# Position bias of the prompt attention added on TensorE by an identity product, with maximum and exponentials read from PSUM

## What is computed

```python
def diff_attention(q, k, v, tq, ts, lam, subln_g, lam_init):
    s = jnp.einsum('bqhjd,bshjd->bhjqs', q, k).astype(jnp.float32) * HEAD_DIM ** -0.5
    dist = jnp.abs(tq[:, None] - ts[None, :]).astype(jnp.float32)
    bias = -alibi_slopes(H_A)[:, None, None] * dist[None]
    mask = (ts[None, :] // CHUNK) <= (tq[:, None] // CHUNK)
    s = jnp.where(mask, s + bias[:, None], NEG)
    p = jax.nn.softmax(s, axis=-1)
    a = p[:, :, 0] - lam * p[:, :, 1]
    o = jnp.einsum('bhqs,bshe->bqhe', a.astype(v.dtype), v)
    o = rms_norm(o, subln_g) * (1.0 - lam_init)
```

## Time and profile before

| what | value |
|---|---|
| median of 3 runs | 1322.1 us (1322.06 to 1329.15) |
| the profiled execution, its own time | 1323.07 us |
| its span, first to last instruction | 1321.3 us |
| mean granted PE clock over the span | 0.917 |
| `attention_prompt`, from PE's first matmul to ACT's last copy | 298.18 to 368.5 us |

### The profile page before, as it was taken

One profiled execution on the slowest core, in us unless ns is written; L12 is line 12 of the kernel. 1 busy time (PEld: TensorE's weight loads), 2 busy tenths in 40 slices (PEclk: granted clock), 3 DMA queues, 4 the chain that ended last, 5 costly groups with the idle time before them and its releaser, 6 DMA issues.

```text
span 1321.3 us, 23547 instructions
## 1 busy us (share of the span) xinstructions
PE 1033.8 (78%) x8385; PEld 657.7 (50%) x8386; DVE 427.7 (32%) x815; ACT 239.2 (18%) x478; POOL 218.1 (17%) x361
## 2 busy tenths in 40 slices
PE   4899899986576699983787788877877878766865
PEld 3888788875565344542344444444433444433432
DVE  4523324338843113874411111111111121101118
ACT  3222212336455000110110101010100111100100
POOL 0002102000100000201222222222231223212211
PEclk9899999996799799997799889899898998978988
DMA  9587666521063793075689699987999988899955
GB/s 350 173 298 256 223 236 216 184 95 48 1 226 112 274 272 115 32 301 201 215 291 386 229 382 395 370 326 272 408 375 387 328 303 299 308 398 404 396 220 216
DMA packets 97912, 347.52 MB, mean 263 GB/s; under 512 B 15057, under 2 KB 20225, under 8 KB 73146
## 3 DMA queue, kind: packets, MB, share of 16 engines
q1 hardware_dynamic: 81258, 311.56, 63.7%
q0 software_dynamic: 13856, 30.13, 6.9%
q10 hardware_dynamic: 2736, 4.98, 1.0%
HBM read 329.15 MB, written 29.52 MB: 271 GB/s over the span
## 4 chain that ended last, share of the span: by engine, by line
PE 27%; DMA 16%; issue 6%; DVE 2%; SPq 1%; ACT 0%; POOL 0%; POOLq 0%; DVEq 0%; ACTq 0%
PE PS L1771 8%; DMA hT<-h_rows,ixo 7%; DMA W<-w 7%; PE PS L1786 6%; PE PS L1802 4%; PE PS L1827 4%; PE PS L1841 2%; PE PS L1777 1%; DMA vec<-ln_b 1%; PE PS L1759 1%; PE PS L1817 1%; DVE hido L1893 0%; PE PS L1794 0%; DVE hid L1888 0%; DMA W<-expert_rows 0%
## 5 line engine op out<-in xcount | busy, mean ns | idle before, releaser
L1771 PE MATMUL PS<-W,XT 128*32 128x256 f32 x2048 | 130.0, 410 | 48.5 <-DMA W<-w 26.5
L1786 PE MATMUL PS<-W,XTo 128*64 128x256 f32 x1216 | 139.5, 381 | 0.0
L1771 PEld LDWEIGHTS PS<-W,XT 128*32 128x32 f32 x2048 | 80.1, 118 | 114.8 <-issue 90.6
L1786 PEld LDWEIGHTS PS<-W,XTo 128*64 128x64 f32 x1216 | 93.2, 137 | 44.0 <-issue 10.6
L1802 PE MATMUL PS<-W,hidTo 128*64 128x512 f32 x304 | 90.7, 722 | 16.3 <-DVE hidTo L1896 10.7
L431 DVE TENSOR_TENSOR w_lo<-raw,w_hi 128x2048 fp32r<-128x2048 f32 x26 | 59.5, 2288 | 126.1 <-ACT w_hi L371 126.1
L305 PE MATMUL PS<-w_hi,u_hi 128*128 128x512 f32 x240 | 94.4, 393 | 1.7 <-DVE w_lo L431 1.7
L305 PE MATMUL PS<-w_hi,u_lo 128*128 128x512 f32 x240 | 93.5, 389 | 0.0
L305 PE MATMUL PS<-w_lo,u_hi 128*128 128x512 f32 x240 | 93.4, 389 | 0.0
L1827 PE MATMUL PS<-W,hidT 128*32 128x512 f32 x512 | 72.1, 677 | 26.3 <-issue 24.3
L1856 ACT ACTIVATE sg<-PS 64x256 f32<-64x256 f32 x32 | 12.1, 378 | 346.9 <-PE PS L1771 346.9
(11 more groups left out here) (338 smaller groups left out, 1497.8 us busy)
## 6 DMA issues: line engine op xcount, KB each, us to landing
W<-w SPq DMA_DIRECT2D x192, 1024.0 KB, 13.9
raw<-w_in SPq DMA_DIRECT2D x26, 1024.0 KB, 9.2
oaT<-w_ada SPq DMA_DIRECT2D x8, 1536.0 KB, 8.6
W<-expert_rows SPq DMA_DIRECT2D x24, 512.0 KB, 12.5
obT<-w_ada SPq DMA_DIRECT2D x8, 512.0 KB, 8.9
kc<-cache_k_diff SPq DMA_DIRECT2D x8, 512.0 KB, 4.8
vc<-cache_v_diff SPq DMA_DIRECT2D x8, 512.0 KB, 3.5
Wa<-p_a SPq DMA_DIRECT2D x4, 1024.0 KB, 7.5
```

Of the source, the lines that this page charges most:

```text
L1771: mm = pe.matmul(PS[64 * h + 32 * c:64 * h + 32 * c + 32, UP_B + i, 0:F], XT[:, i, k, 32 * c:32 * c + 32], t.W13[:, 2 * i + c, h, k], star ...
L1786: mm = pe.matmul(PS[64 * h:64 * h + 64, XH_B, 0:F], XTo[:, k], t.W13[:, slot, h, k], start=k == 0, stop=k == KD - 1)
```

## The change

The scores come out of PSUM complete. Before each product of queries and keys, PE now multiplies the identity (stationary) by the bias (moving, 128 or 256 columns) into the same place of PSUM (`start=True, stop=False`), and the scores are accumulated on it. The factor SM goes into the queries: ACT's eviction of `qT` multiplies by it, and `b_col` is multiplied by it once by a new small DVE instruction, for which ACT waits (`bias_scaled`). In `logits` the two instructions of L773 are gone: the maximum is taken straight from PSUM. The exponentials read PSUM as well and write `L`. With that the waits move: `scores(n)` and `logits(n)` wait for the exponentials of group n-2 (`exp_done`), and the exponentials of group n wait for `a_done` of group n-2, since they are what writes `L` now. In `attention_sample` the multiply-and-add becomes an add.

```diff
--- before.py
+++ after.py
@@ -142,7 +142,7 @@
         ada2_in, ada2_mm, ada2_ev = sem("ada2_in"), sem("ada2_mm"), sem("ada2_ev")
         mod_out = [sem(f"mod2_out{i}") for i in range(2)]
         brow_in = [sem(f"brow_in{i}") for i in range(2)]
-        bin_in = sem("bin_in")
+        bin_in, bias_scaled = sem("bin_in"), sem("bias_scaled")
         g_add, g_sig = sem("g_add"), sem("g_sig")
         g_out = [sem(f"g_out{i}") for i in range(2)]
         hi_done, lo_done, half0_mm = sem("hi_done"), sem("lo_done"), sem("half0_mm")
@@ -396,19 +396,19 @@
                 for m in range(2 * half, 2 * half + 2):
                     act.wait_ge(u_done, m + 1)
                     act.copy(u_hi[:, 2 * m:2 * m + 2], nT[:, 2 * m:2 * m + 2]).then_inc(ut_hi, 1)
-            act.wait_ge(bin_in, 32)
             for c in range(NCH):
                 if c:
                     hi_part(2 * c + 1)
                 hi_part(2 * c + 2)
                 if c == 0:
                     constants.scalar(act)
+                    act.wait_ge(bias_scaled, 1)
                 for n in of_chunk[c]:
                     i = jobs[n][1]
                     if c in QC:
                         act.wait_ge(z_mm, n + 1)
                         u = QC[c] + i
-                        act.activation(t.qT[:, u], PS[:, n % 5, 0:TOK], ACT.Identity, bias=b_col[:, u:u + 1]).then_inc(z_ev_act, 1)
+                        act.activation(t.qT[:, u], PS[:, n % 5, 0:TOK], ACT.Identity, bias=b_col[:, u:u + 1], scale=SM).then_inc(z_ev_act, 1)
                     if c in GC:
                         m = NT * (c - GC[0]) + i
                         act.wait_ge(g_add, m + 1)
@@ -487,6 +487,8 @@
                     lo_part(2 * c + 1)
                 lo_part(2 * c + 2)
                 if c == 0:
+                    dve.wait_ge(bin_in, 32)
+                    dve.tensor_scalar(b_col[:, :], b_col[:, :], SM, None, ALU.mult).then_inc(bias_scaled, 1)
                     constants.vector_early(dve)
                 else:
                     late_mod(c - 1)
@@ -693,13 +695,16 @@
             def scores(n):
                 tile, g = GR[n]
                 S = P * (tile + 1)
+                x0 = P * (1 - tile)
                 if n >= 2:
-                    pe.wait_ge(lg_done, n - 1)
+                    pe.wait_ge(exp_done, n - 1)
                 for hh in range(2):
                     for j in range(2):
                         rows, u = heads(g, j, hh)
-                        mm = pe.matmul(PS[:, 6 * (n % 2) + j, 256 * hh:256 * hh + S], t.qT[rows, u, P * tile:P * tile + P],
-                                       t.kT[rows, u, 0:S], start=True, stop=True)
+                        scored = PS[:, 6 * (n % 2) + j, 256 * hh:256 * hh + S]
+                        bias = t.alibi_p[:, 2 * g + hh, x0:256] if g < 4 else t.band_p[:, 4 * (g - 4) + 2 * hh + j, x0:256]
+                        pe.matmul(scored, t.ident[:, :], bias, start=True, stop=False)
+                        mm = pe.matmul(scored, t.qT[rows, u, P * tile:P * tile + P], t.kT[rows, u, 0:S], start=False, stop=True)
                 mm.then_inc(sc_mm, 1)
 
             def turn(n):
@@ -763,17 +768,12 @@
 
             def logits(n):
                 tile, g = GR[n]
-                S, x0 = P * (tile + 1), P * (1 - tile)
+                S = P * (tile + 1)
                 dve.wait_ge(sc_mm, n + 1)
                 if n >= 2:
-                    dve.wait_ge(a_done, n - 1)
-                for j in range(2):
-                    bias = t.alibi_p[:, 2 * g:2 * g + 2, x0:256] if g < 4 else \
-                        t.band_p[:, :, x0:256].rearrange("p (u j) x -> p u j x", j=2)[:, 2 * (g - 4):2 * (g - 4) + 2, j]
-                    ins = dve.scalar_tensor_tensor(L[:, n % 2, j, :, 0:S], PS[:, 6 * (n % 2) + j].rearrange("p (h x) -> p h x", h=2)[:, :, 0:S],
-                                                   SM, bias, ALU.mult, ALU.add)
-                    link(ins)
-                link(dve.tensor_reduce(mx[:, n % 2], L[:, n % 2, :, :, 0:S], AX.X, ALU.max))
+                    dve.wait_ge(exp_done, n - 1)
+                b0 = 6 * (n % 2)
+                link(dve.tensor_reduce(mx[:, n % 2], PS[:, b0:b0 + 2].rearrange("p j (h x) -> p (j h) x", h=2)[:, :, 0:S], AX.X, ALU.max))
                 dve.tensor_scalar(mx[:, n % 2], mx[:, n % 2], -1.0, None, ALU.mult).then_inc(lg_done, 1)
 
             def weights(n):
@@ -835,10 +835,12 @@
                     tile, g = GR[n]
                     S = P * (tile + 1)
                     act.wait_ge(lg_done, n + 1)
+                    if n >= 2:
+                        act.wait_ge(a_done, n - 1)
                     for j in range(2):
                         for hh in range(2):
                             r = L[:, n % 2, j, hh, 0:S]
-                            ins = act.activation(r, r, ACT.Exp, bias=mx[:, n % 2, 2 * j + hh:2 * j + hh + 1],
+                            ins = act.activation(r, PS[:, 6 * (n % 2) + j, 256 * hh:256 * hh + S], ACT.Exp, bias=mx[:, n % 2, 2 * j + hh:2 * j + hh + 1],
                                                  accum_out=lsum[:, n % 2, 2 * j + hh:2 * j + hh + 1])
                     ins.then_inc(exp_done, 1)
                 if 1 <= n <= len(GR):
@@ -1055,8 +1057,8 @@
                 if b >= 2:
                     dve.wait_ge(pt_mm, b - 1)
                     link(dve.memset(Pn[:, b % 2, :, NF * (b - 2):NF * (b - 2) + NF], 0.0))
-                link(dve.scalar_tensor_tensor(r.rearrange("p g s -> p (g s)"), PS[:, 2 + 4 * (b % 2), 0:3 * SW], SM,
-                                              t.sbias[:, :, :].rearrange("p g s -> p (g s)"), ALU.mult, ALU.add))
+                link(dve.tensor_tensor(r.rearrange("p g s -> p (g s)"), PS[:, 2 + 4 * (b % 2), 0:3 * SW],
+                                       t.sbias[:, :, :].rearrange("p g s -> p (g s)"), ALU.add))
                 link(dve.tensor_reduce(mxs[:, b % 2], r, AX.X, ALU.max))
                 dve.tensor_scalar(mxs[:, b % 2], mxs[:, b % 2], -1.0, None, ALU.mult).then_inc(slg_done, 1)
```

## The result

| | before | changed |
|---|---|---|
| median, us (4 runs each) | 1325.62 (1322.06 to 1332.03) | 1348.31 (1341.42 to 1371.05) |
| ratio | | 1.0171 [1.0131, 1.0210] |
| profiled execution, its span | 1323.07, 1321.3 | 1351.79, 1350.0 |
| first score record to first transpose of the key cache ("the phase") | 298.18 to 368.79 = 70.6 | 299.48 to 397.58 = 98.1 |
| behind the phase | 952.5 | 952.4 |

The change makes the kernel slower by 1.7%. Run once more beside three other kernels, it gave 1.0169 [1.0107, 1.0232], six runs between 1342.6 and 1372.1. The ratios leave out runs that are more than 1.5% above the fastest of their kernel, which are four of the ten runs of the changed kernel, so its median over all ten, 1355.6, lies above what the ratio says.

A forecast was written before the change was run, and what follows sets the result against it. DVE bounds prompt attention before, PE after. The last maximum comes 24.1 us later, some 1.9 us come back: +22.2 on the profiled 1323.07 gives 1345.3, by the median 1344.3; forecast 1345 us, range 1325 to 1356.

The forecast's parts named there:

- rival 3: Prompt attention: PE's clock stays low in tile 1 too, about +53 us, about 1376 us; chance 0.09.
- DVE leads before, and 14.2 us go from it: Prompt attention: DVE sets the pace, and removing the pair at L773 takes 14.2 us from it.
- The maximum and the exponentials from PSUM cost nothing, the moved waits are free: Prompt attention: PSUM reads taken as 0, bounds 0 and 2 us for the maximum; later waits are for work already ended.
- Eight changes a group at 0.20 us (high) and 0.30 (low): PE's scores: each switch between 128-row and 64-row products costs 0.20 us high, 0.30 low; eight a group instead of two.
- The way back: PE's switch from 64-row to 128-row products: bounds 0.04 to 0.20 us at the high clock, taken as 0.20.
- The second rival: Inside a group of scores, switches cost nothing; gain 6 us, 1316 us, limit 1308; chance 0.14.
- Scores of a group and steps of PE: PE: scores 5.0 us high, 9.2 low in tile 1; steps 6.4 (tile 1, high) and 7.1 (tile 0, low).
- The clock low through tile 0 and high from tile 1 on: Prompt attention: PE's clock assumed low through tile 0, high from tile 1; with this the last maximum comes 24.1 us later.
- the fourth rival: PE's clock rises only after tile 1's first group: +3.8 us more, 1349 us; chance 0.50 together with the forecast.
- 1.9 us come back at the end: After the last maximum, PE's 5 us of steps formerly at the low clock run high, returning some 1.9 us.
- the small edits: New DVE instruction on `b_col` hidden, 0 or 0.2 us; scale in ACT's eviction and add in sample attention: 0.

The follow-up runs named there:

- grouped order: Changed kernel with each group's four identity products first, then its four score products, two changes of height a group: 1314.62 us, 0.9953.
- full-height order: Changed kernel in its own order, but each score product takes all 128 rows, which alters the output: phase 63.5 us; total 1331.43 us isn't comparable.
- experiment with the clock held high: Changed kernel with four dense full-height products of 512 columns, results unread, ahead of the first score: 1332.78 us, 1.0055; phase 80.5 us.
- four changes a group: Changed kernel with two identity products, then two score products, twice a group: 1322.48 us, 1.0007; phase 65.6 us.
- unused products: Kernel before with an identity product ahead of each score product, its result not used; DVE's work and old waits kept: 1362.26 us, 1.0273.
- one execution with dense products ahead: Kernel before with unused identity products ahead of its score products and four dense products ahead of the phase: 1341.34 us, 1.0119; this execution's phase 117.9 us.

## Why the prediction was right, and where it was off

The forecast was 1345 us (1325 to 1356), slower; the median is 1348.3, the ratio 1.017. Of the ten runs in the two rounds five lie in the range and five above it, and the median of the second round, 1361.95, is above it, so its upper end was too low. That the first four runs gave so near a number is partly luck: the mechanism was right, but no row told where the clock would rise, and the choice of the place carried some 30 us between rival 3 and the forecast.

- **DVE leads before, and 14.2 us go from it: right.** Without the identity products the phase lost 13.9 us.
- **The maximum and the exponentials from PSUM cost nothing, the moved waits are free: right.** 1225 against 1220 ns; PE's waits are nearly gone; the grouped order has the same waits and is faster than before.
- **Eight changes a group at 0.20 us (high) and 0.30 (low): right, both ways.** A call is 0.725 us in tile 0 (2 x 0.214 + 0.30 = 0.73) and 0.63 in tile 1 (2 x 0.215 + 0.20 = 0.63). The way back, for which I had only 0.04 to 0.20, costs the upper bound, since identity and score products go at one pace. The full-height order shows 0.43 without a change. The second rival (changes are free) is refuted by it.
- **Scores of a group and steps of PE: right.** 9.04 us for 9.2, 6.31 for 6.4, 6.96 for 7.1.
- **The clock low through tile 0 and high from tile 1 on: off by one group.** PE reached tile 1 after 338.17 - 299.48 = 38.7 us, where 39.1 were forecast. Then the first group of tile 1 and the transposes behind it ran at the low clock. This was the fourth rival, at +3.8 us; by the prediction's own costs of a group it would be 9.2 - 5.0 = 4.2. The last maximum, with its negative, was ready 81.6 us after the start of the phase, against 77.4 by the sum and 53.4 before. So the step that failed is "high from tile 1 on", and it accounts for the 4.2 us.
- **1.9 us come back at the end: right where they were looked for, and lost again behind it.** From the last maximum to the end of the phase it takes 98.1 - 81.6 = 16.5 us, where it took 70.6 - 53.4 = 17.2: 0.7 came back. First the changed kernel, then the kernel before:

```profile
382.35 1.09 PE L717 MATMUL PS<-ident,A 128*128 128x128 f32 x8 [1.30 <-DVE A L796]
...
387.40 0.61 PE L750 MATMUL PS<-ident,O 128*128 128x128 f32 x4
...
394.69 1.97 PE L750 MATMUL PS<-ident,O 128*128 128x128 f32 x8 [1.03 <-DVE O L811]
...
394.13:397.58 3.45, 1.97 (x8) 1.60 (x9) 0.50 (x1) 1.32 (x3) 0.00 (x0) 0.50 0.00 0
```

```profile
359.80 0.61 PE L745 MATMUL PS<-ident,O 128*128 128x128 f32 x4
...
366.71 1.09 PE L745 MATMUL PS<-ident,O 128*128 128x128 f32 x8 [0.68 <-DVE O L811]
```

  From the transposes of group 10 to the first transposes of `O`, PE took 387.40 - 382.35 = 5.05 us instead of 359.80 - 352.84 = 6.96, which is the 1.9. From there to the end of the phase it took 10.2 us instead of 9.0. The clock had fallen again at 394.13, and the last eight transposes took 1.97 us instead of 1.09; the prediction had no such fall.

- Together +27.5 in the phase for +22.2. The 1.3 us ahead of it are within the spread of where the phase begins, so they neither bear out nor refute the bounds of 0 to 0.2 for the small edits.

What I had underrated is the clock. I wrote the changes as the cause and the clock as a condition. The experiment with the clock held high gives 4.7 us to the new order at the high clock (11.8 to its changes, less what it gains) and 22.8 to the low clock. The changes leave PE empty for 0.30 of each 0.73 us at the low clock, and they are also what goes together with it: with two or four changes a group, or with none at the same interleaving, it rose 4 to 12.5 us after the start; with eight it rose after 50 us, and after 86 with the unused products. Whether the empty times are what holds the clock down, or the 64-row products that stand alone with half of the array unused, isn't shown: the full-height order takes away both, and the orders with two and four changes keep their pairs. My third rival, the clock low in tile 1 too, had 0.09; it is what the 86 us show in a sister kernel, and four of the ten runs of the changed kernel, 1364.5 to 1372.1 us, come near its 1376. It would have deserved more, with a range up to there.

## What to carry to other kernels

A 64-row product between two of 128 rows cost PE 0.20 us each way at the high clock and 0.30 at the low one, with 128 and with 256 columns. So put products of one height together, here four identity products with one `start` per bank and then the scores, which stand in pairs again: the same arithmetic goes from 1.7% slower to 0.5% faster. Read a "busy" PE against its clock and the distance from start to start: in the row with 50 us of busy PE at clock 0.50, a product of tile 0 streamed for 0.43 of each 0.73 us. Before moving work from DVE to PE, work out PE's step in the new order, not only the time of the added products.

## What the runs showed of the hardware

- **A clock that stays low without any wait.** PE had no wait in the first 50 us of the phase and the clock stayed at 0.50; with unused products 86 us. By the distances from start to start it had only short empty times, 0.30 us at each change of height. In the full-height order, with as many products in the same order, the clock was at 1.00 after 4 us.
- **A clock lost in busy work.** In one execution with dense products ahead it fell from 1.00 to 0.50 with no wait longer than 0.33 us just before, and stayed there for 71 us.
- **Exponentials from PSUM.** 480 ns for 256 columns against 496 from SBUF, but the read of the accumulator behind it 209 against 187 ns; together no gain.
- **Spread behind the phase.** The experts' part took between 686 and 699 us in profiles of kernels with the same scores, and the part from the key cache to the experts 260 to 267; a change of 5 us is hard to see in the whole time of this kernel, and plain in the phase.
